# Between the stages of a two-layer transformer kernel: residual and norm by token tile, the norm's root applied on TensorE by a diagonal matrix, norm weights as scales of the PSUM evictions

## The reference, cut to what matters

```
def rms_norm(x, g):
    y = x * rsqrt(mean(x * x, -1, keepdims=True) + 1e-6)
    return y * g

x = x + rms_norm(mla_mixer(rms_norm(x, g0)), g1)       # site 0 -> x1
x = x + rms_norm(conv_ffn(rms_norm(x, g2)), g3)        # site 1 -> x2
x = x + rms_norm(diff_mixer(rms_norm(x, g4)), g5)      # site 2 -> x3
x = x + rms_norm(conv_ffn(rms_norm(x, g6)), g7)        # site 3 -> x4
# third layer: a mixer with w_in_2 (attention with an index of chosen keys, gates), then
# a router and 32 experts, of which each token takes two; then a last norm
```

## Time and profile before

| | us |
|---|---|
| three timed runs | 1344.73, 1347.19, 1347.28; median 1347.19 |
| the profiled execution | 1345.34 |
| its span | 1343.5 (1.84 us lie around the span) |
| PE busy | 1282.8 (95% of the span) |
| granted TensorE clock, mean of the span | 0.994 |
| HBM read | 339.1 MB |

### The profile page before, as it was taken

One profiled execution on the slowest core, in us unless ns is written; L12 is line 12 of the kernel. 1 busy time (PEld: TensorE's weight loads), 2 busy tenths in 40 slices (PEclk: granted clock), 3 DMA queues, 4 the chain that ended last, 5 costly groups with the idle time before them and its releaser, 6 DMA issues.

```text
span 1343.5 us, 20032 instructions
## 1 busy us (share of the span) xinstructions
PE 1282.8 (95%) x7959; PEld 954.6 (71%) x7959; DVE 509.6 (38%) x1303; ACT 548.0 (41%) x853; POOL 573.2 (43%) x136
## 2 busy tenths in 40 slices
PE   6999999999998899999999999999999999999996
PEld 6867999998987799999878888854444444454442
DVE  2434444445265454444657453421111111121112
ACT  4654555556477465555543664311111111111112
POOL 4722788885944188888567855200000000000001
PEclk9999999999999999999999999999999999999998
DMA  8731666664633266664446444599999999999994
GB/s 270 235 94 63 182 195 188 190 199 144 220 126 95 63 203 196 196 188 165 149 165 203 159 137 161 230 421 426 427 428 428 429 428 429 429 429 428 429 423 189
DMA packets 156933, 341.22 MB, mean 254 GB/s; under 512 B 8537, under 2 KB 119482, under 8 KB 144314
## 3 DMA queue, kind: packets, MB, share of 16 engines
q1 hardware_dynamic: 156858, 340.18, 68.1%
HBM read 339.10 MB, written 1.05 MB: 253 GB/s over the span
## 4 chain that ended last, share of the span: by engine, by line
PE 75%; DMA 13%; ACT 4%; DVE 4%; POOL 2%; issue 1%; SPq 0%; ACTq 0%; DVEq 0%
PE bank L669 16%; PE bank L671 15%; PE bank L670 15%; PE bank L1237 11%; DMA xspare<-in_w 6%; DMA ring<-in_w 6%; PE bank L1262 5%; PE bank L1187 3%; PE bank L768 2%; POOL parts L621 2%; PE bank L679 1%; PE bank L1217 1%; ACT parts L1305 1%; PE bank L1105 1%; PE bank L1121 1%
## 5 line engine op out<-in xcount | busy, mean ns | idle before, releaser
L621 POOL TENSOR_TENSOR parts<-raw,parts 128x2048 fp32r<-128x2048 f32 (+4 forms) x128 | 568.0, 4466 | 290.2 <-ACT parts L1305 290.2
L669 PE MATMUL bank<-xh,parts 128*128 128x256 f32 x1032 | 288.0, 279 | 6.0 <-POOL parts L621 4.0
L670 PE MATMUL bank<-xl,parts 128*128 128x256 f32 x1032 | 285.9, 277 | 0.0
L671 PE MATMUL bank<-xh,parts 128*128 128x256 f32 x1032 | 285.8, 277 | 0.0
L1305 ACT ACTIVATE parts<-raw 128x2048 fp32r<-128x2048 f32 (+4 forms) x128 | 236.1, 1853 | 23.4 <-PE bank L669 8.5
L1237 PE MATMUL bank<-ring,room 128*64 128x512 f32 x768 | 226.1, 594 | 7.1 <-DMA ring<-in_w 4.5
L644 POOL TENSOR_TENSOR xn<-h,gpost 128x512 f32<-128x512 f32 x4 | 4.9, 1270 | 474.7 <-DVE h L2258 474.7
L669 PEld LDWEIGHTS bank<-xh,parts 128*128 128x128 f32 x1032 | 194.2, 188 | 12.6 <-POOL parts L621 4.8
L670 PEld LDWEIGHTS bank<-xl,parts 128*128 128x128 f32 x1032 | 193.8, 188 | 0.8
L671 PEld LDWEIGHTS bank<-xh,parts 128*128 128x128 f32 x1032 | 193.9, 188 | 0.0
L1237 PEld LDWEIGHTS bank<-ring,room 128*64 128x64 f32 x768 | 72.5, 137 | 111.4 <-issue 111.4
(11 more groups left out here) (255 smaller groups left out, 1858.9 us busy)
## 6 DMA issues: line engine op xcount, KB each, us to landing
ring<-in_w SPq DMA_DIRECT2D x67, 2048.0 KB, 22.9
raw<-in_ffn_w_up SPq DMA_DIRECT2D x88, 512.0 KB, 4.9
room<-in_w SPq DMA_DIRECT2D x12, 2048.0 KB, 20.3
raw<-in_ffn_w_down SPq DMA_DIRECT2D x44, 512.0 KB, 3.9
xspare<-in_w SPq DMA_DIRECT2D x11, 2048.0 KB, 26.6
raw<-in_w_in SPq DMA_DIRECT2D x40, 512.0 KB, 4.1
raw<-in_diff_w_qkv SPq DMA_DIRECT2D x24, 512.0 KB, 4.6
ring<-in_w SPq DMA_DIRECT2D x10, 1024.0 KB, 24.8
```

Of the source, the lines that this page charges most:

```text
L621: pool.tensor_tensor(low[:, p % PARTS, 0:n], raw[:, p % RING, 0:n], high[:, p % PARTS, 0:n], ALU.subtract).then_inc(low_ready, 1)
L669: first = pe.matmul(out_, a[0], b[0], start=start, stop=False)
L670: pe.matmul(out_, a[0], b[1], start=False, stop=False)
L671: return first, pe.matmul(out_, a[1], b[0], start=False, stop=stop)
```

## The change

- A new tensor gcol holds the norm weights of x1 to x4, a column for each k-tile. They come in by four small DMAs of 8 rows with the convolution's parameters, and by the transposition that already turned these. Four of the six loads of gpre are gone, and the waits of SP with them.
- `post` becomes `turned_over`: gain, sum, root and residual of tile 0, then the same of tile 1; ACT's guess too is made by tile. The last piece of `down` has the tile outside: both banks of tile 0 end before those of tile 1.
- `normed` becomes `spread_roots`: for each tile the root of h is multiplied into an identity matrix (spread_r, 128x128, in score). PE makes h^T * diag(root) as a plain f32 product, 8 for each tile, so that h itself is the stationary operand (`h_transposed`). Two k-tiles with both token tiles fill a bank.
- ACT evicts xh per k-tile, 128x256, with the norm weight as scale (`high_chunks`), and DVE the low part (`low_chunks`); it waits until ACT has done both k-tiles of a bank. PE waits for bank q at k-tile 2q.
- At x4 h is transposed directly, without root or weight, tile 0 as soon as its residual is in h.
- `keep_clock` has 23 products instead of 32; at x4 there are 5 ahead of tile 0 and 11 between the tiles.
- x4 and qi lie in banks 0 to 3.

```diff
             def pre_gains(n, src):
 
                 if n:
-                    sp.wait_ge(xn_ready, 4 * n)
+                    sp.wait_ge(xn_ready, 4)
...
             rows_on(prow[0:1, 4, :], A["diff_subln_g"][0])
-            pre_gains(1, A["norm_g"][0, 2])
+            for x, src in enumerate((A["norm_g"][0, 2], A["norm_g"][1, 0], A["norm_g"][1, 2], A["g_mix_2"][0])):
+                rows_on(prow[1 + KT * x:1 + KT * x + KT, 4, :], src)
...
+            def h_transposed(name, site, scaled, between=0):
+                b = [begin(G[name] + q) for q in range(4)]
+                for t in range(NT):
+                    if t and between:
+                        keep_clock(between, bank[4])
+                    if scaled:
+                        pe.wait_ge(spread_ready, 2 * (site - 1) + t + 1)
+                    else:
+                        pe.wait_ge(h_ready, 2 * (site - 1) + t + 1)
+                    for k in range(KT):
+                        at = S * (k % 2) + P * t
+                        dst, src = b[k // 2][:, at:at + P], h[:, t, P * k:P * k + P]
+                        if scaled:
+                            ins = pe.matmul(dst, src, spread_r[:, t], start=True, stop=True)
+                        else:
+                            ins = pe.transpose(dst, src, ident)
+                        if t == 0 and k == 0:
+                            behind(ins)
+                        if t and k % 2:
+                            end(ins, G[name] + k // 2)
+                late.extend([(2 * q, G[name] + q) for q in range(4)])
...
-            WAIT = 32
+            WAIT = 23
...
-                if k == 4:
-                    while late:
-                        moved(pe, late.pop(0))
+                while late and late[0][0] <= k:
+                    moved(pe, late.pop(0)[1])
...
+                    each = [(x, t, hf) for x in range(2) for t in range(NT) for hf in range(2)]
+                    if stop:
+                        each = [(x, t, hf) for t in range(NT) for x in range(2) for hf in range(2)]
...
             keep_clock(WAIT, begin(G["x1"]))
-            x_transposed("x1", 1)
+            h_transposed("x1", 1, True)
...
-            keep_clock(WAIT, bank[3])
-            x_transposed("x4", 4)
+            keep_clock(WAIT // 4, bank[3])
+            h_transposed("x4", 4, False, WAIT // 2)
...
+            def high_chunks(name, site):
+                for k in range(KT):
+                    g = G[name] + k // 2
+                    full(act, g)
+                    act.activation(xh[:, k, :], bank[BANK[g]][:, S * (k % 2):S * (k % 2) + S], ACT.Copy,
+                                   scale=gain_of(site, k)).then_inc(x_high, 1)
...
+            def low_chunks(name, site):
+                for k in range(KT):
+                    g = G[name] + k // 2
+                    x_parts[0] += 1
+                    dve.wait_ge(x_high, x_parts[0] + (1 - k % 2))
+                    ins = dve.scalar_tensor_tensor(xl[:, k, :], bank[BANK[g]][:, S * (k % 2):S * (k % 2) + S],
+                                                   gain_of(site, k), xh[:, k, :], ALU.mult, ALU.subtract)
...
+                def residual(t):
+                    root_of(t, st[:, 16 + t:17 + t])
+                    for g in (ring_groups or [])[2 * t:2 * t + 2]:
+                        moved(dve, g)
                     dve.scalar_tensor_tensor(h[:, t, :], xn[:, t, :], st[:, 16 + t:17 + t], h[:, t, :],
                                              ALU.mult, ALU.add).then_inc(h_ready, 1)
+                dve.wait_ge(gpost_here, 16 * (site + 1))
+                gained_half(0, 0)
+                summed(0)
+                gained_half(0, 1)
+                residual(0)
+                gained_half(1, 0)
+                summed(1)
+                gained_half(1, 1)
+                residual(1)
+            def spread_roots(site):
+                for t in range(NT):
+                    dve.wait_ge(h_squares, 2 * site + t + 1)
+                    half_of(t, st[:, t:t + 1])
+                    root_of(t, st[:, 28 + t:29 + t])
+                    dve.tensor_scalar(spread_r[:, t], ident, st[:, 28 + t:29 + t], None, ALU.mult).then_inc(spread_ready, 1)
```

More of the change, by code:

```diff
@@ L192, in plan @@
     groups("diff_t3", 1, [2])
-    for name, n in [("x3", 4), ("x4", 4), ("qi", 4), ("row", 1), ("qa", 2), ("qi_t", 2),
+    groups("x3", 4)
+    groups("x4", 4, [0, 1, 2, 3])
+    groups("qi", 4, [0, 1, 2, 3])
+    for name, n in [("row", 1), ("qa", 2), ("qi_t", 2),
                     ("ki_t", 1), ("ka", 2), ("qa_t", 2), ("index", 8), ("va", 2), ("ka_t", 2), ("qb", 2), ("kb", 2),
@@ L930, in down @@
                     w = parts(p, 2, D)
[L931 to L941, removed]
+                    each = [(x, t, hf) for x in range(2) for t in range(NT) for hf in range(2)]
+                    if stop:
+                        each = [(x, t, hf) for t in range(NT) for x in range(2) for hf in range(2)]
+                    for i, (x, t, hf) in enumerate(each):
+                        if not any(x == y for y, _, _ in each[:i]):
+                            pe.wait_ge(hid_ready, n + (n0 + 1 + x))
+                        first, ins = product(bank[4 + 2 * t + hf][:, :],
+                                             [y[:, (j + x) % 4, t * P:t * P + P] for y in (hh, hl)],
+                                             [y[:, x, 512 * hf:512 * hf + 512] for y in w],
+                                             start and x == 0, stop and x == 1)
+                        behind(first)
+                        if stop and x == 1:
+                            ins.then_inc(ffn_full, 1)
                     owed[0] += 1
@@ L1318, in h_sums @@
             def h_sums(site, dst=16, junk=None):
+                by_tile = 0 < site < 4
                 for t in range(NT):
@@ L1324, in h_sums @@
                     squares(st[:, t:t + 1], h[:, t, :], xn[:, t, :] if junk is None else view(junk + D * t, D), h_squares)
-                act.wait_ge(h_squares, 2 * site + 2)
-                guess(st[:, dst:dst + 2], st[:, 0:2], D)
+                    if by_tile:
+                        act.wait_ge(h_squares, 2 * site + t + 1)
+                        guess(st[:, 28 + t:29 + t], st[:, t:t + 1], D)
+                if not by_tile:
+                    act.wait_ge(h_squares, 2 * site + 2)
+                    guess(st[:, dst:dst + 2], st[:, 0:2], D)
             def guess(dst, sums, width):
@@ new lines, in turned_over, with gained_half, summed @@
+            def turned_over(site, banks, ring_groups):
+                def gained_half(t, hf):
+                    b = banks[2 * t + hf]
+                    dve.wait_ge(post_squares, 4 * site + 2 * t + hf + 1)
+                    x = slice(512 * hf, 512 * hf + 512)
+                    ins = dve.tensor_tensor(xn[:, t, x], bank[b][:, :], gpost[:, x], ALU.mult)
+                    ins.then_inc(bank_moved[b] if ring_groups else vec, 1)
+                    if not ring_groups:
+                        steps[0] += 1
+                def summed(t):
+                    dve.wait_ge(post_squares, 4 * site + 2 * t + 2)
+                    dve.tensor_tensor(st[:, 18 + t:19 + t], st[:, 2 + 2 * t:3 + 2 * t], st[:, 3 + 2 * t:4 + 2 * t],
+                                      ALU.add).then_inc(sums_ready, 1)
+                    dve.wait_ge(sums_ready, 2 * site + t + 1)
+                    half_of(t, st[:, 18 + t:19 + t])
+                def residual(t):
+                    root_of(t, st[:, 16 + t:17 + t])
+                    for g in (ring_groups or [])[2 * t:2 * t + 2]:
+                        moved(dve, g)
@@ L1948, in _ @@
                 moved(dve, g)
-            post(0, [BANK[G["mla_o"] + n] for n in range(4)], range(G["mla_o"], G["mla_o"] + 4))
+            turned_over(0, [BANK[G["mla_o"] + n] for n in range(4)], range(G["mla_o"], G["mla_o"] + 4))
             def tile(n, b, par):
@@ L1985, in _ @@
             ffn(0)
-            post(1, range(4, 8), None)
+            turned_over(1, range(4, 8), None)
             x_transposed("x2", 2)
```

106 lines of the change are left out of this document (48 added, 58 removed).

## The result

| kernel | median us | lowest to highest | executions |
|---|---|---|---|
| before | 1346.38 | 1344.73 to 1347.28 | 4 |
| after | 1356.6 | 1353.46 to 1358.74 | 4 |

The ratio is 1.0073, 95% interval 1.0056 to 1.009: slower by 10 us, where the forecast was 8.8 us faster. The profiled execution took 1353.46 us with a span of 1351.7.

The account below looks back on a forecast made before the run. PE bounds the kernel, busy 95% of the span and 75% of the chain; four gaps give 2.2 + 1.3 + 2.2 + 3.1 = 8.8 us of 1345.34: 1336.5, or 1338.4 from the median; put at 1337.6, range 1334 to 1342.

Parts of the forecast that it names:

- T: Start of the filling products at each of the four sites; the gap runs from there to PE's next useful matmul.
- Costed at nothing: New `down` order, four small DMAs (about 1.2 us in SP's queue), wider transposition and small copy: nothing in the sum.
- the order: Last `down` piece asks for its second k-tile 1.4 us earlier: a hole of 0 to 0.3 us at worst.
- Tile by tile: At x1, tile 0's residual starts 0.38 us before the fillers; ACT squares tile 1 1.3 us earlier.
- root as a product: At x1, products of 1.87 us per tile replace the xn halves; tile 1 follows tile 0 without a hole.
- evictions: At x1, ACT's two end at 129.09, DVE's at 129.93; PE starts at 130.0, not 132.47; 2.2 us, likewise x3.
- x2: POOL, at work until 316.06, delays tile 0's residual by 0.9 us: gain 1.3 us instead of 2.2.
- x4: Fillers hold PE until 654.71; with fewer, PE starts at 654.2 instead of 657.37: gain 3.1 us.
- Rival (a): Behind x4 or at an FFN's start, PE's gain turns into waits for POOL: 5.7 saved, 1341 us; chance 0.17.
- Rival (c): A plain f32 product costs four transpositions, not two, 3.7 us a tile: 1.7 slower, 1348 us; chance 0.02.
- Rival (b): Clock falls at each site, from fillers' end into the next stage: 7 us slower, 1353 us; chance 0.04.

## Why the prediction was wrong

The gaps, T to the first product behind it:

| | x1 | x2 | x3 | x4 | sum against before |
|---|---|---|---|---|---|
| before | 11.97 | 11.97 | 11.97 | 9.94 | |
| predicted | 9.5 | 10.4 | 9.5 | 6.8 | -9.6 (-8.8 in its sum) |
| after | 9.59 | 11.75 | 9.59 | 7.43 | -7.5 |
| gcol last, scalar column | 9.75 | 10.63 | 9.75 | 7.02 | -8.7 |

- **The step that failed** stands in no sentence: the sum set everything outside the four gaps at nothing, and *Costed at nothing* lists the order, the DMAs and the copy, but not the tensor gcol itself. With the tensor alone the kernel was 18 us slower, of which 14 at an equal clock; the forecast gain was 8.8. With the tensor out of the way, allocated last, the time is 1341.66, inside the range of 1334 to 1342 at its upper edge, and the gain 4.3, half of the forecast. Nothing in the trace of before gave the price of the place, but before's own trace had both levels: in 133 to 143 us its 256-column products lie 0.118 apart, in 147 to 156 they lie 0.113 apart, at a clock of 1.00. I had read durations of single operations there and not their distance.
- **Tile by tile, root as a product, evictions** were right: 2.38 for 2.2 at x1 and x3. T - 0.47 for T - 0.38 at the first residual, 3.74 us for 32 records, 0.36 of spacing on ACT for 0.38. One reading was off and harmless: four gains in 2.68 us are 0.66 apart, not 0.60; the changed kernel has 0.60 from a gain to the instruction behind it at x1. Tile 1's products follow tile 0's without a hole, as put.
- **x2**: POOL's hold was foreseen, on the wrong instruction. I let the residual wait, which comes after the root. The sum ahead of it has two SBUF inputs too, is held first, and holds back guess and root. The prediction's own times had it there: the sum starts 0.3 + 0.60 + 0.55 ahead of the residual, at 313.7, and POOL ends at 316.06. The gain was 0.22 and not 1.3; with the sum freed it is 1.34, and the residual is then held as predicted (1.77 us, 1.1 behind POOL).
- **x4**: 2.51 for 3.1. POOL, until 653.3 (640.78 + 12.52), held the sum here as well (0.66 us for 0.15); 2.92 with the sum freed.
- **Rival (a)**, waits for POOL: POOL's share of the chain stays at 2%, and PE's products waited 6.8 us in all for POOL's low parts where before they waited 6.7. **Rival (c)** is refuted by the 3.74 us. **Rival (b)**: in all four gaps of the changed kernel's trace the clock was 1.00. But executions with gcol last had a lower mean clock (0.991 in seven of ten, where the middle of before's 14 beside them was 0.9935; 0.0025 of 1340 us is 3.3 us), which is enough for the 2.2 us that its gain fell short of its gaps; in the traces, with the falls taken out, it is 7.6 us ahead of before. That the change causes this is not shown, and the runs don't agree: the changed kernel with 32 fillers ran at a median of 0.995 and with 23 at 0.991, but the tensor alone, with before's gaps and 32 fillers, at 0.9905, with falls behind both pauses.
- In the order, no hole stood at the last `down` piece.

What stays open: by which mechanism the place of operands sets the distance of products, why the level changes at some pauses and between executions, and which pair of tensors decides. The place of hh and hl (with st and what lies behind them) matters, since the 512-column products go wide with it. That of xh and xl wasn't moved alone: the shift that adds them, and wr, br, lamp, h, xn and xspare, makes all the 256-column products wide. Room and score don't matter.

## What to carry to other kernels

A new tensor is an edit by itself: allocate it behind the tensors that the matmuls read, and time it once alone. When PE is busy all the time at a clock of 1.00 and still gets through fewer products in a window, compare the starts of equal products in both traces before looking for waits. In these traces DVE instructions with two SBUF inputs, from 128x1 to 128x1024, waited for POOL's operation to end, so look for the first such one in a chain, not for the largest.

## What the hardware showed that I had not expected

- The distance of fp32r products in a stream has levels: 0.1133, 0.1178 and 0.120 us for 256 columns, about 0.229 and 0.2335 for 512, all at a clock of 1.00. A shift of the tensors behind gcol by 64 or 128 bytes per partition widened the 256-column ones (128 bytes the 512-column ones too), for some 14 us of 1346 at an equal clock with the tensor alone; 512 bytes didn't.
- With one placement (256 bytes) the same kernel ran at either level, 1344.0 and 1333.3 us of span, in series on two chips.
- An addition of 128x1 took 2.35 us beside POOL, and 0.21 with its second input as a scalar column.
- The kernel with the column last, the scalar column and the fillers in the pause took 1337.83 us, and the one with 256 bytes of pad and no such fillers 1335.93 in its second series: 0.993 and 0.9927 of before.
